# A hybrid decoder layer with 16 experts on one core: splitting each expert's weights in four chunks, and letting products wait for the chunk they read

## The reference

```
proj = x @ w_in                          # -> u, q, k, v
a = differential attention(q, k, v)      # 4 heads, causal, ALiBi
s = S5 scan(u), GELU, GLU
x = layer_norm(alpha * x + concat(a, s) @ w_out)
gates = route(x)                         # sigmoid scores, one of 4 groups, top 2 of its 4 experts
for e in range(16):                      # moe_w_gate, moe_w_up: 1024 x 512; moe_w_down: 512 x 1024
    h = silu(x @ w_gate[e]) * (x @ w_up[e])
    out += gates[:, e] * (h @ w_down[e])
x = layer_norm(alpha * x + out)
```

## Time and profile before

| | us |
|---|---|
| median of 3 runs | 1306.68 |
| lowest and highest of them | 1303.94, 1307.88 |
| the profiled execution's own time | 1303.61 |
| span of its trace | 1301.5 |

### The profile page before, as it was taken

The page is one execution under the profiler, slowest core; times in us unless marked ns, Lnnn a source line. Parts: engine busy times, 40 slices in busy tenths (PEclk is TensorE's granted clock), DMA queues, the critical chain, the costliest instruction groups (busy, mean ns, idle before and its releaser), DMA issues. The chain is left out here.

```text
span 1301.5 us, 17352 instructions
## 1 busy us (share of the span) xinstructions
PE 1094.6 (84%) x5512; PEld 895.8 (69%) x5513; DVE 689.7 (53%) x1287; ACT 515.4 (40%) x752; POOL 325.7 (25%) x541
## 2 busy tenths in 40 slices
PE   7998999995998695989996258999999999999720
PEld 5886788993666584577774247888888888778510
DVE  3653735503888112445443835544447678675527
ACT  4232321424777312521111043544446567465313
POOL 0807184402000100000000011334233543445315
PEclk9998999996999866988897578999999999999965
DMA  6132221117600402632221074666778799987434
GB/s 223 41 105 53 91 53 50 33 23 278 192 1 1 151 1 72 216 152 97 97 89 54 0 290 157 228 207 206 236 237 309 252 310 411 351 274 245 109 127 164
DMA packets 51249, 201.33 MB, mean 155 GB/s; under 512 B 9107, under 2 KB 15635, under 8 KB 45043
## 3 DMA queue, kind: packets, MB, share of 16 engines
q1 hardware_dynamic: 40674, 138.43, 30.0%
q0 software_dynamic: 7488, 27.27, 8.6%
q10 hardware_dynamic: 3024, 34.87, 6.9%
HBM read 163.81 MB, written 36.73 MB: 154 GB/s over the span
## 5 line engine op out<-in xcount | busy, mean ns | idle before, releaser
L2014 DVE TENSOR_TENSOR wlo<-raw,whi 128x4096 fp32r<-128x4096 f32 x48 | 211.5, 4423 | 95.7 <-ACT whi L1943 95.6
L1943 ACT ACTIVATE whi<-raw 128x4096 fp32r<-128x4096 f32 x48 | 174.9, 3649 | 93.2 <-SPq L1816 38.7
L1852 POOL DMA_INDIRECT acc<-eyb,idxs x25 | 68.1, 2722 | 156.8 <-ACT eyb L1961 156.8
L1885 PE MATMUL psY<-whi,ehs 128*128 128x512 f32 x200 | 82.1, 411 | 9.7 <-DVE wlo L2014 9.7
L1885 PE MATMUL psG<-whi,exs 128*128 128x512 f32 x200 | 83.3, 416 | 4.5 <-DVE exs L2019 4.4
L1887 PE MATMUL psG<-whi,exs 128*128 128x512 f32 x200 | 80.8, 404 | 0.0
L1886 PE MATMUL psG<-wlo,exs 128*128 128x512 f32 x200 | 80.8, 404 | 0.0
L1886 PE MATMUL psY<-wlo,ehs 128*128 128x512 f32 x200 | 79.9, 400 | 0.0
L1887 PE MATMUL psY<-whi,ehs 128*128 128x512 f32 x200 | 79.8, 399 | 0.0
L1885 PE MATMUL psU<-whi,exs 128*128 128x512 f32 x200 | 79.3, 396 | 0.0
L1886 PE MATMUL psU<-wlo,exs 128*128 128x512 f32 x200 | 79.2, 396 | 0.0
(11 more groups left out here) (389 smaller groups left out, 2481.8 us busy)
## 6 DMA issues: line engine op xcount, KB each, us to landing
raw<-in_moe_w_gate SPq DMA_DIRECT2D x16, 2048.0 KB, 8.8
raw<-in_moe_w_up SPq DMA_DIRECT2D x16, 2048.0 KB, 16.7
raw<-in_moe_w_down ACTq DMA_DIRECT2D x16, 2048.0 KB
w_raw<-in_w_in SPq DMA_DIRECT2D x27, 256.0 KB, 3.2
stg<-in_x_prompt SPq DMA_DIRECT2D x8, 512.0 KB, 4.3
kc<-in_cache_k SPq DMA_DIRECT2D x16, 256.0 KB, 3.0
vc<-in_cache_v SPq DMA_DIRECT2D x16, 256.0 KB, 3.0
raw<-in_x_prompt SPq DMA_DIRECT2D x8, 512.0 KB, 6.4
```

The source lines that it names most:

```text
L1852: nc.gpsimd.indirect_dma_start(s.acc, bass.IndirectOffsetOnAxis(ap=idxs[:, 0:1], axis=0), yb[j][:, :], None, compute_op=ALU.add).then_inc( ...
L1885: pe.matmul(out, hi, w_hi, start=(k == 0), stop=False)
L1943: nc.scalar.activation(whi[:, at], s.raw[:, at], ACT.Copy).then_inc(hi_made[i], 1)
L2014: nc.vector.tensor_tensor(wlo[:, at], s.raw[:, at], whi[:, at].bitcast(F32), ALU.subtract) \
```

## The change

Each piece of 4096 columns is rounded by four ACT instructions of 1024 columns instead of one, and its remainder made by four DVE instructions; each increments its semaphore. `hi_made` and `lo_made` count quarters instead of pieces, so they start from 4, and all waits on them and `split_by` are scaled by 4. DVE's quarter waits for ACT's quarter. PE's gate and up products wait for a quarter at every second step and the first half of the down product at every step, in place of one wait for the whole piece ahead of the product. Loads and their buffers are as before: SP and ACT issue the next load when all four quarters of the old piece are made. Routing has one small DVE instruction more.

```diff
--- before.py
+++ after.py
@@ -1720,7 +1720,8 @@
                 ch(nc.vector.tensor_reduce(eb[:, 0:E], among, AX.X, ALU.add))
                 ts(s.order[:, :], eb[:, 0:E], E - 1.0, None, ALU.min)
                 ch(ts(w0[:, 0:1], top[:, :], 1.0, None, ALU.add))
-                ch(ts(s.split_by[:, :], count[0:1, 0:E], ne[:, 0:1], w0[:, 0:1], ALU.add, ALU.min))
+                ch(ts(eb[:, 0:E], count[0:1, 0:E], ne[:, 0:1], w0[:, 0:1], ALU.add, ALU.min))
+                ch(ts(s.split_by[:, :], eb[:, 0:E], 4.0, None, ALU.mult))
 
                 ch(tt(A(past), wide(count[0:1, 0:NSB + 1], E), mid(end[0:1, :], NSB + 1), ALU.is_ge))
                 ch(tt(A(past), A(past), mid(ne[:, :], NSB + 1), ALU.mult))
@@ -1806,6 +1807,11 @@
 
             return type(b) is not int or b >= n
 
+        def quarter(i, c):
+
+            a, n = PIECES[i][0], (PIECES[i][1] - PIECES[i][0]) // 4
+            return slice(a + n * c, a + n * (c + 1))
+
         def entry(eng, row, b, lo, hi):
             return eng.value_load(s.wtab[0:1, row, bass.ds(b, 1)], min_val=lo, max_val=hi)
 
@@ -1818,7 +1824,7 @@
                 sp.dma_start(s.lb2[:, :], io["ln2_b"].to_broadcast([P, D])).then_inc(l_in, 16)
                 with sp.Fori(1, E) as r:
                     e = sp.value_load(s.order[0:1, bass.ds(r, 1)], min_val=0, max_val=E - 1)
-                    free = sp.value_load(s.split_by[0:1, bass.ds(r, 1)], min_val=1, max_val=E + 1)
+                    free = sp.value_load(s.split_by[0:1, bass.ds(r, 1)], min_val=4, max_val=4 * E + 4)
                     for i in range(2):
                         sp.wait_ge(w_in[i], 16 * r)
                         sp.wait_ge(lo_made[i], free)
@@ -1876,10 +1882,12 @@
                         last = pe.transpose(psX[:, k * P:(k + 1) * P], xv[:, k, :], s.ident[:, :])
                     last.then_inc(x_turned, 1)
 
-                def product(out, x, steps, at):
+                def product(out, x, steps, at, wait_for=None):
 
 
                     for k in range(steps):
+                        if wait_for is not None and k % (steps // 4) == 0:
+                            wait_for(k // (steps // 4))
                         hi, lo = (part[:, k * P:(k + 1) * P] for part in x)
                         w_hi, w_lo = (part[:, at(k):at(k) + 512] for part in (whi, wlo))
                         pe.matmul(out, hi, w_hi, start=(k == 0), stop=False)
@@ -1888,14 +1896,14 @@
                     return last
 
                 def gate_up(b, j):
-                    count = entry(pe, 1, b, 1, E) + 1
-                    pe.wait_ge(lo_made[0], count)
+                    done = 4 * entry(pe, 1, b, 1, E) + 1
                     pe.wait_ge(x_split, b + 1)
                     if from_block(b, 1):
                         pe.wait_ge(act_done, b)
-                    product(psG[:, :], xs[j], KD, lambda k: GATE_AT + k * FE).then_inc(g_made, 1)
-                    pe.wait_ge(lo_made[1], count)
-                    product(psU[:, :], xs[j], KD, lambda k: UP_AT + k * FE).then_inc(gu_made, 1)
+                    product(psG[:, :], xs[j], KD, lambda k: GATE_AT + k * FE,
+                            lambda c: pe.wait_ge(lo_made[0], done + c)).then_inc(g_made, 1)
+                    product(psU[:, :], xs[j], KD, lambda k: UP_AT + k * FE,
+                            lambda c: pe.wait_ge(lo_made[1], done + c)).then_inc(gu_made, 1)
 
                 def turn_h(b, j):
                     pe.wait_ge(act_done, b + 1)
@@ -1908,14 +1916,14 @@
 
                 def down(b, j):
 
-                    count = entry(pe, 1, b, 1, E) + 1
-                    pe.wait_ge(lo_made[2], count)
+                    done = 4 * entry(pe, 1, b, 1, E) + 1
                     pe.wait_ge(h_split, b + 1)
                     if from_block(b, 1):
                         pe.wait_ge(y_kept, b)
                     for half in range(2):
                         last = product(psY[:, half * 512:half * 512 + 512], hs[j], KF,
-                                       lambda k: DOWN_AT + k * D + half * 512)
+                                       lambda k: DOWN_AT + k * D + half * 512,
+                                       (lambda c: pe.wait_ge(lo_made[2], done + c)) if half == 0 else None)
                     last.then_inc(y_made, 1)
 
                 turn_x(0, 0, 1)
@@ -1939,8 +1947,9 @@
                     act.wait_ge(w_in[i], 16 * entry(act, 0, b, 1, E))
                     if after is not None:
                         act.wait_ge(*after)
-                    at = slice(*PIECES[i])
-                    nc.scalar.activation(whi[:, at], s.raw[:, at], ACT.Copy).then_inc(hi_made[i], 1)
+                    for c in range(4):
+                        at = quarter(i, c)
+                        nc.scalar.activation(whi[:, at], s.raw[:, at], ACT.Copy).then_inc(hi_made[i], 1)
 
                 def keep_x(b, j):
                     act.wait_ge(x_turned, b + 1)
@@ -1964,6 +1973,8 @@
                     e = act.value_load(s.order[0:1, bass.ds(r, 1)], min_val=0, max_val=E - 1)
                     act.dma_start(s.raw[:, slice(*PIECES[2])], expert_weights(io, e, 2)).then_inc(w_in[2], 16)
 
+                for i in range(3):
+                    act.sem_inc(hi_made[i], 4)
                 high(0, 0)
                 keep_x(0, 0)
                 load_down(0)
@@ -1985,7 +1996,7 @@
                         with act.If(entry(act, 3, b - 1, 0, 1) > 0):
 
                             r, count = entry(act, 0, b - 1, 1, E - 1), entry(act, 1, b - 1, 1, E)
-                            act.wait_ge(lo_made[2], count + 1)
+                            act.wait_ge(lo_made[2], 4 * count + 4)
                             load_down(r)
                     keep_x(b + 1, 1 - j)
                     with act.If(new > 0):
@@ -2009,10 +2020,12 @@
             def _(dve):
                 def low(b, i):
 
-                    at = slice(*PIECES[i])
-                    dve.wait_ge(hi_made[i], entry(dve, 1, b, 1, E))
-                    nc.vector.tensor_tensor(wlo[:, at], s.raw[:, at], whi[:, at].bitcast(F32), ALU.subtract) \
-                        .then_inc(lo_made[i], 1)
+                    before = 4 * entry(dve, 1, b, 1, E)
+                    for c in range(4):
+                        at = quarter(i, c)
+                        dve.wait_ge(hi_made[i], before + c + 1)
+                        nc.vector.tensor_tensor(wlo[:, at], s.raw[:, at], whi[:, at].bitcast(F32), ALU.subtract) \
+                            .then_inc(lo_made[i], 1)
 
                 def low_x(b, j):
                     dve.wait_ge(x_kept, b + 1)
@@ -2020,7 +2033,7 @@
                         .then_inc(x_split, 1)
 
                 for i in range(3):
-                    dve.sem_inc(lo_made[i], 1)
+                    dve.sem_inc(lo_made[i], 4)
                 low(0, 0)
                 low_x(0, 0)
                 low(0, 1)
```

## The result

| | before | after |
|---|---|---|
| median, us | 1305.31 (4 runs, 1300.55 to 1307.88) | 1291.92 (4 runs, 1283.98 to 1294.83) |
| ratio | | 0.9889, 95% interval 0.9846 to 0.9932 |
| profiled execution | 1303.61 | 1292.0 |
| span of its trace | 1301.5 | 1289.9 |
| first gate product to end of last down product | 483.46 | 469.17 |

The change makes the kernel faster by 1.1%. The forecast was 1293.2 us, a ratio of 0.9897 to the median of the runs it started from; the range 1285.5 to 1301.5 holds the median.

What follows compares the result with a forecast made beforehand. PE was taken to bound the experts' stage, so splitting pays only where PE stands still for it. 4.7 + 3.0 + 5.8 = 13.5 us off the median 1306.68 gives 1293.2 us, range 1285.5 to 1301.5.

Steps and rivals of the forecast that it cites:

- Term 1: PE's 8.90 us gap before the first turn of h: 2.37 from overlap plus 2.36 from earlier down weights, 4.7 us.
- cold clock: Gate product behind the first gap starts at 1.2 instead of 2.4 GHz after PE stood still; forecast left it unchanged.
- Term 2: Four short waits of gate products for split activations, at experts with one block, all vanish: 3.0 us.
- Term 3: Last down product starts on its first ready quarter, near 1231.2 instead of 1236.98: 5.8 us earlier.
- PE's added waits: 225 more register-value waits in PE's gate, up and down products, taken to cost 0; other end 20 us.
- Price of one split: ACT's rounding plus DVE's subtraction of one piece: 8.07 us whole, 5.70 in quarters, ready 2.37 earlier.
- warm case: At the last down product, the clock stays up in the shorter gap: gain 6.5 us instead of 5.8.
- D: Rival, slower: PE pays 0.09 us for each added wait, 20 us on and 13.5 off, 1313; chance 0.08.
- E: Rival: DVE becomes the bound in the one-block stretch, 7.5 us gain left, 1299.2; chance 0.09.
- C: Rival: DMA stays late, first-gap gain 2.4 and short-wait gain 0; 8.2 us in all, 1298.5; chance 0.17.
- B: Rival: down load gains about twice as much, clock holds at first gap; 17.9 us in all, 1288.8; chance 0.18.

Runs made afterwards that it cites:

- g4: The kernel before the change, unchanged, profiled once more: stretch from first gate product to end of last down product 486.02 us; ACT starts first down piece at 13.37.
- e2: Kernel before, pieces still worked whole, plus the changed kernel's 12 PE waits per block: stretch 483.80 us, ratio 1.0013.
- f1: Changed kernel with SP's loads of the second expert held until the first down weights have landed: stretch 465.74 us, ratio 0.9848.
- e3: Changed kernel with SP's second-expert loads held until the first tokens are turned; gate load issued 1.0 us behind the down load: stretch 468.98 us, ratio 0.9904.
- c8: Changed kernel with eighths of 512 columns in place of quarters, and waits to match: stretch 472.34 us, ratio 0.9903.
- f2: Changed kernel with the second expert's gate load held back to 0.5 us ahead of the first down load: stretch 475.49 us, ratio 0.9931.
- e4: Changed kernel with only down pieces in quarters, gate and up pieces whole as before: stretch 475.01 us, ratio 0.9907.
- e1: Changed kernel, but PE waits once ahead of a product for all four quarters: stretch 472.14 us, ratio 0.9946 to before.
- g2: f1 once more, with more rounds, beside the changed kernel on the same chip: 1285.93 us, ratio 0.9859, stretch 465.47 us.
- d1: Changed kernel with ACT's first down load issued ahead of the copy of the first tokens: stretch 465.72 us, ratio 0.99.

## Why the prediction was right

| term | forecast, us | measured in the stretch, us |
|---|---|---|
| 1, gap near the start | 4.7 | 5.4, and 0.7 of cold clock |
| 2, short waits | 3.0 | 3.0 |
| 3, the end | 5.8 | 5.6, less 0.4 of cold clock |
| PE's added waits | 0 | 0 |
| sum | 13.5 | 14.3 |

The sum is of one pair of profiles, and its closeness is in part luck of that pair: from g4's stretch, 486.02 us, the changed kernel's three profiles lie 16.9 to 17.2 us away. With e2, 483.80, as a third profile without split pieces, the gain is 14.3 to 17.2 us, and the forecast of 13.5 lies a little under all of them.

**Price of one split: right.** 5.70 us were worked out from neighbours, and in the gap it is 776.51 + 4.63 - 775.42 = 5.72. DVE's four quarters take 4.63 us for 4.42 and ACT's 3.90 for 3.62. The Trainium skill's 58 cycles for every further instruction (VectorE: DVE Perf Modes, section The TRN2 errata) at 0.96 GHz make 0.18 us for three more, an estimate; the trace has 0.21.

**Term 1: right for this kernel, with a reason that doesn't carry further.** The overlap gave its 2.4 us, 8.07 - 5.72. The other 3.1 us are the earlier down start, 14.31 to 11.19, where 2.36 were forecast. The step said that the work in front of the down load is done earlier. It is: the gate load is issued 4.1 us ahead of the first gate product instead of 1.9, and the packets show what came of it (view under f1): when the down load's first packet starts, 107 of the gate load's packets have started, and 48 before. The 59 packets between them are 0.96 MB, and at the 418 GB/s of the earlier trace rows that is 2.3 us, an estimate. The rest, 0.8 us, is within what profiles of one kernel differ by: down start is 13.37 in g4 and 10.71 to 11.26 in the changed kernel.

What the step left out is that nothing need be in front of the down load at all. It suggests that any later gate load is worse, and e3, built on that, refuted it: with the gate load 1.0 us behind, down start is 10.69. What costs most is that both loads are issued within half a microsecond. With the gate load 2.4 us ahead or 1.0 behind the down weights come 2 to 5 us earlier (c8 excepted), and with SP's loads out of the way (f1) another 3. How the engines choose between the packets of two queues stays open. The Trainium skill, DMA: Bandwidth & Descriptors, section Issuing engines are not separate DMA queues, says that transfers started by different engines run on the same 16 DMA engines and interleave; f2 against f1, 15.91 to 8.41 in down start, agrees with that.

The cold clock was left as it was. It moved a little both ways: the gate product behind the gap took 6.92 us instead of 7.61, the last down product 8.05 instead of 7.64. In both the granted clock was at the lower of its levels at first, for about 3.4 us from 783.0 on and for about 4.8 us of the last product. These are the windows around the end of the gap, which ends at 782.52 (columns as above):

```profile
782.00:783.00 1.00, 0.48 (x4) 0.48 (x4) 1.00 (x2) 0.00 (x0) 0.30 (x2) 1.00 0.51 82
783.00:784.00 1.00, 0.63 (x4) 0.35 (x3) 0.60 (x1) 0.59 (x1) 0.00 (x0) 0.52 0.70 242
```

After the last turn of h PE stood still only 4.1 us instead of 9.7 and the product still started cold, so the 6.5 us that the warm case would have given weren't there. In f1, where PE stood still 0.8 us, the product was warm.

**Term 2: right.** All four short waits went. e4 shows that it takes quarters in the gate and up pieces as well. Profiles of kernels with whole pieces differ in these losses (3.0 us before, 4.4 in e2, 5.5 in g4), so the term was read from the mildest of them: that it came out to the tenth is luck, that it is at least 3 us is not.

**Term 3: right.** PE started 2.71 us after ACT's first quarter, 2.52 were worked out. e1 shows that 3.4 us of it belong to PE's waits and the other 2.2 to the overlap.

**The rivals.** D was refuted by e2. E was refuted by the changed kernel and by c8: DVE busy 16.93 of 18.20 us, PE without a wait. The Trainium skill, Perfetto Trace Analysis, section Optimizing Scalar/DVE Operations, allows either outcome by whether the engine is saturated; at 0.93 busy it wasn't. C had DMA as the late one: the DMA share is 1.02 in that window of the changed kernel and PE still has no wait. B came halfway: more than 2.4 us from the landing, but no warm clock. f1 is B: its stretch is 17.7 us shorter than before, B had 17.9.

**The times.** The forecast took 3.1 us as the distance of the profiled execution from the median. The profiled pair differs by 11.6 us, and the measured ratio gives 0.0111 x 1305.31 = 14.5, next to the stretch's 14.3.

## What to carry to other kernels

An engine pair that works on a large piece one after the other costs time only where somebody waits for that piece, here at the first, the last and the tightest places; count those places, as in this kernel the gain of splitting was there and nowhere else. Waits that were already true cost nothing here (e2), so giving the consumer one for every part it reads is worth trying. Look at what else becomes earlier when a step is made shorter: here a load that nobody needed for 30 us was the one that delayed the load everybody waited for, and holding it back by one line was worth as much again as the waits per quarter.

## What the runs showed of the hardware

- Two loads of 2 MB issued within 0.5 us by SP and ACT: ACT starts on the one waited for 14.9 to 17.6 us after its issue (before, g4, e2, e4, f2). With the other load 2.3 to 2.7 us ahead or 1.0 behind: 12.1 to 13.0 (c8: 15.9). With no other load: 9.8 to 10.1 (f1, g2).
- The first packet of the down load starts 1.1 us behind its issue in f1, where no other load is under way, and 3.7 us behind it in the changed kernel, where the gate load is 2.4 us ahead.
- A wait whose value comes from a register costs PE nothing when it is already true: with 225 more, a block still takes 18.17 us (e2).
- DVE's subtraction takes 0.68 us in mean for 512 columns (c8), 1.22 for 1024 and 4.42 for 4096; back to back, four of 1024 take 0.21 us longer than one of 4096 (4.63 and 4.42).
- A DMA that stands behind ACT's work in the program is issued while that work still runs, if it has nothing to wait for: in d1 at 754.57 us, while ACT rounds a piece from 753.76 to 757.66; the tokens' gather beside it was then 6.5 us late.
